# Reordering the halves of an output projection, and the router's work between them, in a kernel that then streams expert weights

## The reference

```
for layer in range(2):
    h = h + hybrid_mixer(rms_norm(h, norm1_g[layer]), w_in[layer], ..., w_out[layer], lb)
    h = h + expert_choice_ffn(rms_norm(h, norm2_g[layer]), w_router[layer], w_gate[layer], w_up[layer], w_down[layer])

hybrid_mixer:       concatenate([r_out, h_out]) @ w_out            # (256x1024) @ (1024x1024)
expert_choice_ffn:  affinity = softmax(xn @ w_router)              # 16 experts
                    gate, idx = top_k(affinity.T, 32)              # each expert takes 32 tokens
                    ye = (silu(xe @ w_gate) * (xe @ w_up)) @ w_down * gate
```

## Time and profile before

| what | value |
|---|---|
| median of 3 runs | 1852.26 us (1852.26 to 1853.85) |
| profiled execution | 1853.35 us, of which the span of instructions is 1851.6 us |
| TensorE matmuls busy | 1454.8 us (79%) |
| VectorE busy | 799.2 us (43%) |
| ScalarE busy | 571.6 us (31%) |
| mean granted TensorE clock | 0.904 of full |
| DMA mean | 304 GB/s over the span |

### The profile page before, as it was taken

One profiled execution on the slowest core, in us unless ns is written; L12 is line 12 of the kernel. 1 busy time (PEld: TensorE's weight loads), 2 busy tenths in 40 slices (PEclk: granted clock), 3 DMA queues, 4 the chain that ended last, 5 costly groups with the idle time before them and its releaser, 6 DMA issues.

```text
span 1851.6 us, 24842 instructions
## 1 busy us (share of the span) xinstructions
PE 1454.8 (79%) x10541; PEld 1070.4 (58%) x10541; DVE 799.2 (43%) x1246; ACT 571.6 (31%) x898; POOL 62.1 (3%) x56
## 2 busy tenths in 40 slices
PE   8999999999999999985645545579999555545556
PEld 7999999999999898861212112149886121111212
DVE  5767777776777799720101001019973010000101
ACT  4555555465555575321000000028532100000001
POOL 1010000010000000100000000002010000000000
PEclk9999999999999999998877777789999877777868
DMA  9426555534655385899999999997479999999997
GB/s 327 143 77 220 196 170 173 174 102 170 198 170 179 130 254 170 304 365 430 430 430 430 430 430 430 429 392 238 159 292 368 429 430 429 430 430 430 430 430 316
DMA packets 165493, 563.14 MB, mean 304 GB/s; under 512 B 12601, under 2 KB 116535, under 8 KB 137607
## 3 DMA queue, kind: packets, MB, share of 16 engines
q1 hardware_dynamic: 155318, 551.49, 76.3%
q10 hardware_dynamic: 10064, 10.06, 1.8%
HBM read 558.05 MB, written 1.05 MB: 302 GB/s over the span
## 4 chain that ended last, share of the span: by engine, by line
PE 52%; issue 23%; DMA 17%; DVE 4%; ACT 2%; SPq 1%; POOL 0%; PEldq 0%; ACTq 0%; POOLq 0%; DVEq 0%
PE psum L2682 6%; PE psum L2976 5%; PE psum L2721 5%; PE psum L2659 5%; PE psum L2661 5%; PE psum L2660 5%; DMA ring<-in_w_down 3%; DMA ring<-in_w_up 3%; DMA ring<-in_w_gate 3%; PE psum L2711 3%; PE psum L2831 2%; DMA arena<-in_w_up 2%; DMA arena<-in_w_down 2%; PE psum L2576 2%; PE psum L2785 2%
## 5 line engine op out<-in xcount | busy, mean ns | idle before, releaser
L2976 PE MATMUL psum<-ring,arena 128*32 128x512 f32 (+1 forms) x1600 | 280.1, 691 | 200.7 <-DMA ring<-in_w_down 77.4
L2976 PE MATMUL psum<-arena 128*32 128x512 f32 x1024 | 206.6, 700 | 147.4 <-DMA ring<-in_w_up 40.5
L2976 PEld LDWEIGHTS psum<-ring,arena 128*32 128x32 f32 x1600 | 70.2, 128 | 349.3 <-issue 346.7
L907 DVE TENSOR_TENSOR W<-ring,W 128x2048 fp32r<-128x2048 f32 (+1 forms) x92 | 206.4, 2243 | 85.9 <-ACT W L888 85.4
L2274 DVE TENSOR_TENSOR arena<-arena,psum 128x512 f32<-128x512 f32 x16 | 11.0, 689 | 452.8 <-PE psum L2976 452.8
L2659 PE MATMUL psum<-XT,W 128*128 128x256 f32 x704 | 199.4, 283 | 0.0
L2661 PE MATMUL psum<-XT,W 128*128 128x256 f32 x704 | 199.1, 283 | 0.0
L2660 PE MATMUL psum<-XT,W 128*128 128x256 f32 x704 | 199.0, 283 | 0.0
L888 ACT ACTIVATE W<-ring 128x2048 fp32r<-128x2048 f32 (+1 forms) x92 | 172.2, 1872 | 79.5 <-PE psum L2661 42.5
L2976 PEld LDWEIGHTS psum<-arena 128*32 128x32 f32 x1024 | 50.1, 126 | 248.6 <-issue 248.6
L2660 PEld LDWEIGHTS psum<-XT,W 128*128 128x128 f32 x704 | 134.9, 192 | 0.9
(11 more groups left out here) (341 smaller groups left out, 2622.2 us busy)
## 6 DMA issues: line engine op xcount, KB each, us to landing
ring<-in_w_down SPq DMA_DIRECT2D x36, 2048.0 KB, 29.8
ring<-in_w_up SPq DMA_DIRECT2D x32, 2048.0 KB, 31.2
ring<-in_w_up SPq DMA_DIRECT2D x58, 1024.0 KB, 5.2
ring<-in_w_gate SPq DMA_DIRECT2D x28, 2048.0 KB, 33.5
ring<-in_w_in SPq DMA_DIRECT2D x54, 1024.0 KB, 7.6
arena<-in_w_up SPq DMA_DIRECT2D x24, 2048.0 KB, 32.8
arena<-in_w_down SPq DMA_DIRECT2D x20, 2048.0 KB, 29.9
arena<-in_w_gate SPq DMA_DIRECT2D x20, 2048.0 KB, 29.7
```

Source lines behind the costliest of these rows:

```text
L907: nc.vector.tensor_tensor(W2[split_pair(v)][:, c], slot(v % SLOTS_1)[:, c], W1[split_pair(v)][:, c].bitcast(F32), ALU.subtract).then_inc(r ...
L2976: last = nc.tensor.matmul(psum[CAP * e:CAP * (e + 1), b, 0:cols.stop - cols.start], src[:, 4 * half + k, CAP * e:CAP * (e + 1)], tiles[e][ ...
```

## The change

Five things change, in both layers of the second model.

- TensorE's order of the halves: before 0 1 2 3, 4 5 6 7; after 0 1 2, 4 5 6, 3 7. The splits on ScalarE and VectorE follow (`OUT_ORDER`), and the places in `out_w1` too.
- `turn_raw(2)` and `raw_logits(1)` go from behind half 7 to between halves 3 and 7.
- `raw_logits(2)` goes from behind `turn_raw(3)` to ahead of it.
- The last split on VectorE goes from ahead of the loop of additions to behind the first addition.
- Home 5 is loaded behind piece 19, homes 6 and 7 behind piece 20.

```diff
-OUT_HOMES = {5: (18, 2), 6: (19, 4), 7: (19, 4)}
+OUT_HOMES = {5: (19, 3), 6: (20, 4), 7: (20, 4)}
+OUT_ORDER = [0, 1, 2, 4, 5, 6, 3, 7]
+OUT_STEP = {n: step for step, n in enumerate(OUT_ORDER)}
...
# ScalarE, round_out(n)
-                    else:
-                        act.wait_ge(proj2, past(proj2) + len(ITEMS) + n - 4 + 1)
+                    if OUT_STEP[n] >= 4:
+                        reader = OUT_ORDER[OUT_STEP[n] - 4]
+                        if reader < 4:
+                            act.wait_ge(proj2, past(proj2) + len(ITEMS) + reader + 1)
+                        else:
+                            act.wait_ge(wo_mm, past(wo_mm) + reader - 4 + 1)
...
# VectorE
-                for n in range(4, 8):
+                for n in OUT_ORDER[4:7]:
                     rest_of_out(n)
...
                     nc.vector.tensor_tensor(dst, psum[:, 4 + i, :].rearrange("p (t n) -> p t n", t=TT), dst,
                                             ALU.add).then_inc(x_mid, 1)
-                    if i:
+                    if i == 0:
+                        rest_of_out(OUT_ORDER[7])
+                    else:
                         turn_raw_dve(i - 1)
                 turn_raw_dve(3)
...
# TensorE
-                for i in range(4):
+                for i in range(3):
                     project_half(i).then_inc(proj2, 1)
...
                 for i in range(4):
+                    if i == 3:
+                        project_half(3).then_inc(proj2, 1)
+                        release(None, 0, [])
+                        turn_raw(2)
+                        raw_logits(1)
                     project_half(4 + i).then_inc(wo_mm, 1)
                     release(wo_mm, past(wo_mm) + i + 1, [mixer_slot(lay, N_IN2 + i)])
-                    if i:
+                    if i in (1, 2):
                         turn_raw(i - 1)
-                    if i >= 2:
-                        raw_logits(i - 2)
+                    if i == 2:
+                        raw_logits(0)
+                raw_logits(2)
                 release(None, 0, [])
                 turn_raw(3)
-                raw_logits(2)
                 raw_logits(3).then_inc(logits, 1)
```

More of the change, by code:

```diff
@@ L815, in out_first @@
         def out_first(n):
-            return out_w1[:, SLOT_W // 2 * (n % 4):SLOT_W // 2 * (n % 4 + 1)]
+            at = OUT_STEP[n] % 4
+            return out_w1[:, SLOT_W // 2 * at:SLOT_W // 2 * (at + 1)]
         def turn_mixed_act(act, past, b, nth):
@@ L1523, in round_out @@
                         in_slot(s)
-                    else:
-                        act.wait_ge(proj2, past(proj2) + len(ITEMS) + n - 4 + 1)
+                    if OUT_STEP[n] >= 4:
[4 more added lines that the diff above has]
+                            act.wait_ge(wo_mm, past(wo_mm) + reader - 4 + 1)
                     nc.scalar.activation(out_first(n), slot(s)[:, out_half(n)], ACT.Copy).then_inc(rounded, 1)
-                for n in range(4):
+                for n in OUT_ORDER[:4]:
                     round_out(n)
@@ L1544, in _ @@
                 turn_mixer_act(act, past, 1, 3)
-                round_out(4)
+                round_out(OUT_ORDER[4])
                 turn_mixer_act(act, past, 3, 1)
-                for n in range(5, 8):
+                for n in OUT_ORDER[5:]:
                     round_out(n)
@@ L2169, in rest_of_out @@
                     s = mixer_slot(lay, N_IN2 + n % 4)
-                    dve.wait_ge(rounded, past(rounded) + N_IN2 - SPLIT_FROM + n + 1)
+                    dve.wait_ge(rounded, past(rounded) + N_IN2 - SPLIT_FROM + OUT_STEP[n] + 1)
                     nc.vector.tensor_tensor(rounded_slot[s][:, out_half(n)], slot(s)[:, out_half(n)], out_first(n).bitcast(F32),
                                             ALU.subtract).then_inc(rest, 1)
-                for n in range(2):
+                for n in OUT_ORDER[:2]:
                     rest_of_out(n)
@@ L2188, in _ @@
                 turn_mixer_rest(dve, 1, 3, xt_act, past(xt_act) + 3)
-                rest_of_out(2)
+                rest_of_out(OUT_ORDER[2])
                 dve.wait_ge(mix_rms, past(mix_rms) + 2)
@@ L2197, in _ @@
                     last.then_inc(mix_done, 1)
-                rest_of_out(3)
+                rest_of_out(OUT_ORDER[3])
                 turn_mixer_dve(dve, past, 2, 0)
@@ L2822, in project_half @@
                     i, ks = n % 4, range(4, 8) if n < 4 else range(4)
-                    pe.wait_ge(rest, past(rest) + N_IN2 - SPLIT_FROM + n + 1)
+                    pe.wait_ge(rest, past(rest) + N_IN2 - SPLIT_FROM + OUT_STEP[n] + 1)
                     w1 = out_first(n).rearrange("p (k n) -> p k n", k=4)
```

## The result

The changed kernel takes 1859.96 us (median of 6 runs, 1858.46 to 1862.81) against 1852.05 (6 runs, 1851.36 to 1853.85) of the kernel before: ratio 1.0042, 95% interval 1.0032 to 1.0053. It is slower by 7.9 us. The forecast was 4.8 us, with a range that just holds the measured median.

The account below looks back on a forecast made before the run. The expert stream is DMA-bound, so the layer's end follows the chain through the logits to loads 22 and 23. 2 x 2.4 = 4.8 us, other terms 0, gave a median of 1857.1 us, range 1853.8 to 1860.2.

Parts of the forecast that it names:

- What bounds, and what carries the shift: Expert stream bound by DMA bytes; the layer's end moves with loads 22 and 23, hence with the chain from projection to first product.
- The first hole: DMA gap from 786 to 800, 3.9 us missing per layer; rival that filling it gives up to 7.8 us, chance 0.05.
- Reordered halves and moved split at 0: Projection on TensorE and its splits: reordering and moved split cost 0, covered by margins.
- turn_raw(2) and raw_logits(1) ahead of half 7: End of projection on TensorE: half 7 ends 1.24 us later, and these items no longer cover the waits on VectorE.
- raw_logits(2) ahead of turn_raw(3): Behind half 7: TensorE and VectorE strictly in turn, two waits of about 1.6 and 1.0 us; logits 2.4 us later per layer.
- The clock: TensorE's granted clock around the logits: a fall costs 0.60; bounds 0.6 less to 0.6 more, plus up to 1.28 per layer.
- one fall, as now, so 0: Clock term as taken: a fall in one of the two layers, as in the kernel before, adding 0 us.
- The clock rival: Clock falls in both layers, on the logits as well: 8.0 us slower, 1860.2 us; chance 0.12.
- the likeliest case: Serial chain behind half 7 as worked out, 4.8 us slower, own range 1856 to 1859; chance 0.70.
- The bound of 1.28 us for a fall on the logits: Most that a clock fall on raw_logits(3) and turn_raw(3) adds in each layer.
- Piece 7: Load queued behind homes 6 and 7: lands at 817.8, wanted at 818.5 by the product with pair 1, margin 0.7, price 0.
- free up to 4.9 us of stream: Late piece 7 costs nothing until its lateness exceeds loads 22 and 23, 4.9 us of stream; rival counted with the chain.

Follow-up runs that it names:

- e3: Changed kernel with VectorE's copy of quarter 2 ahead of the addition of quarter 3: 1857.57 us, ratio 1.0026.
- e8: Kernel before with only the changed load order (home 5 behind piece 19, homes 6 and 7 behind piece 20): 1855.56 us, ratio 1.0017.
- e12: e8 with 5 idle products ahead of the product with pair 1: 1853.62 us, ratio 1.0008.
- e1: Changed kernel with turns and logits back where they were, homes 6 and 7 behind piece 19, new order of halves and splits kept: 1852.04 us, ratio 0.9997.
- e6: Changed kernel with raw_logits(2) back behind turn_raw(3) and homes 6 and 7 behind piece 19: 1855.93 us, ratio 1.0017.
- e7: Kernel before with one edit, raw_logits(2) ahead of turn_raw(3): 1856.73 us, ratio 1.0020.
- e9: e4 with homes 6 and 7 behind piece 19 and more idle products (17 under choice of tokens, 2 behind marked rows): 1857.38 us, ratio 1.0024.
- e10: The changed kernel run again, unaltered: 1860.75 us, ratio 1.0041.
- e2: Changed kernel with homes 6 and 7 loaded behind piece 19 again: 1860.12 us, ratio 1.0038.
- e5: Changed kernel with the edits of e3 and e2 together: 1855.04 us, ratio 1.0014.
- e11: e1 with the 17 and 2 idle products of e9: 1852.38 us, ratio 0.9998.
- e4: Changed kernel with 5 idle products ahead of raw_logits(2) and 3 ahead of raw_logits(3): 1861.31 us, ratio 1.0045.

## Why the prediction was right or wrong

**What bounds, and what carries the shift: right.** Load 22 and 23 to the layer's end is the same to 0.4 us in each layer of all kernels but e3, e8 and e12. The first hole was worth nothing (e1).

**Reordered halves and moved split at 0: right**, e1: no wait of L2840 on a split of the weights, 25.57 us as before.

**turn_raw(2) and raw_logits(1) ahead of half 7: right**, 1.33 us measured where 1.24 were taken.

**raw_logits(2) ahead of turn_raw(3): right in mechanism and size.** Counted from the end of half 7 (0.20 ahead of the addition), raw_logits(2), VectorE's last copy and raw_logits(3) start at 1.55, 3.13 and 3.88; the prediction has 1.57, 3.06 (801.97 less 0.69, from 798.22) and 3.84. raw_logits(3) gives way to the idle products at 4.79, not at 4.65. So the logits come 1.33 + 1.21 = 2.54 us later in a layer, not 2.4. e3, e6 and e7 show the waits and the swap one by one. The 1.21 us arise only where raw_logits(2) stands ahead of turn_raw(3) and VectorE's copy of quarter 2 behind the addition: with either put back (e3, e6) the stretch is 3.3 us, and what stays is the 1.33 of the turns less 0.25.

**The clock: this is the term that was mis-sized.** The prediction took "one fall, as now, so 0". The chain without it is 5.1 us; less the 0.6 that the kernel before pays for its own fall that is 4.5, and e9, where the clock doesn't fall in this stretch, measures 4.7. The change as it is measures 7.9 and 8.0. In both profiles of the changed kernel the clock falls in both layers, on the logits in three of the four cases at 0.3, 1.1 and 1.5 us, and at 0.2 to 0.6 in each layer behind them. That makes 1.9 us in one profile and 3.0 in the other, so 1.3 and 2.4 more than before. The second of these executions is at the median, and there the falls are nearly all that is missing. The first is 1.5 us under its median, and what the slower runs around it pay for is not shown. The clock rival, with 0.12, gave 8.0 us by the same mechanism: falls in both layers, partly on the logits. The measured time is the rival's and not that of the likeliest case, though it agrees to 0.1 us in part by luck: the rival's chain was 0.3 us too short and its falls too dear. For the same reason the range held only just. The bound of 1.28 us for a fall on the logits was still a little low for one case: raw_logits(2)'s end and turn_raw(3) fell into it in e10, 1.53.

The Trainium skill (TensorE: Matmul & The Clock Gate, Part 4: PE-mode transpose) had it that transposes don't count as work. The runs agree with the direction that it gave: the stretch with turns, thin products and waits brought falls in both layers, 5.4 to 8 us by that sentence and 7.9 measured. They don't separate the turns from the rest. In the kernel before TensorE ran turns and products with 16 columns without a wait, and the clock fell behind them in the first layer but not in the second; and in e9 the same turns and thin products, with the waits filled, brought no fall in either.

**Piece 7: its landing was mis-sized by 1.4 us, and its price is not general.** Forecast was a landing 14.7 us behind the issue of piece 20 and a margin of 0.7. The product with pair 1 starts 818.02 - 801.91 = 16.1 behind it, 1.2 later than it otherwise could. What the 1.4 us are, the runs don't separate; the queue was empty ahead of piece 20 (0 GB/s from 800 to 802). In the changed kernel this costs nothing that shows (e2), as forecast. In the kernel before the same line costs 3.0 us by the medians and 2.4 behind load 22 in the first layer (e8), and with the copy first 2.5 by the medians (e3 against e5). The rule "free up to 4.9 us of stream" was wrong: it counted two loads and forgot those that wait for the last gather, and it took no account of the clock in the late product. Why the changed kernel escapes is not shown by a run of its own. Its profiles have the fall ahead of that product and not in it, and 13.1 us from load 22 to the arena loads in the first layer, under the 14.6 of cover, as the 12.4 in the second layer of e8.

**Open.** Where the clock falls differs between executions of one kernel, and there is one profile for each but two for the change; so the shares of single runs are not known. e3's second layer ends 1.0 us late behind load 22 without a fall in the products around piece 7; the cause is open. So is what e12 would show with piece 7 no later than in e8.

## What to carry to other kernels

In a hand-ordered kernel ask of each reordering what stood between a producer and its consumer in every stream: here the two moved items were the cover for two VectorE copies, and a consumer placed ahead of the turn that feeds the other engine makes both engines take turns. A hole in the DMA is worth filling only if no later hole waits for something else. Where TensorE waits or does thin work ahead of a serial stretch, price the fall of its clock in every layer, and look where it goes: here filler in the two waits moved the fall to a dearer place, and of the versions tried only filler throughout got rid of it. Even so that version is 4.7 us slower than the kernel before: no run here makes the new order pay.

## What the runs showed of the hardware

The kernel before, first layer, around its fall:

```profile
798.00:800.00 2.00, 2.00 (x20) 1.92 (x19) 1.23 (x3) 1.98 (x5) 0.26 (x1) 1.00 0.92 365
800.00:802.00 2.00, 2.00 (x14) 2.00 (x14) 0.61 (x4) 0.94 (x6) 0.43 (x1) 0.65 0.95 393
```

- There the clock fell after a stretch in which the profile has TensorE busy without a gap, with turns and 16-column products: granted clock 1.00 from 798 to 800, 0.65 from 800 to 802, 0.50 from 802 to 804. The same work in the second layer was followed by no fall (1.00 from 1406 to 1408).
- From the logits through the product with pair 1 the clock fell in one of the two layers in the profiles of the kernel before, e1, e6 and e11; in both layers in those of the changed kernel, e2 to e5, e7, e8, e10 and e12; and in none in e9.
- A fall cost 0.2 to 0.8 us ahead of the first expert product when it came in the softmax (changed kernel 13.22, e11 13.76, against 13.0), 0.3 to 1.5 on the logits (e10), 1.4 on the gather and the first product (e4, 14.38). Where it lay in a product that was late already, the layer ended 2.1 to 2.5 us later (e3, e8, e12, first layers against 423.1), lateness and the hole in DMA included.
- From the end of VectorE's copy to the start of the waiting product on TensorE 0.06 us passed (797.75 + 0.68 to 798.49), near the lower of the two bounds that the prediction took.
